# A hybrid decoder layer on one core: the block-sharing product goes ahead of the transposes of L and lv, and half of the masked score copies go behind it

## The chip, the cores and the metric

The kernel runs on one core of one Trainium2 chip. The metric is the time of one execution on the device in microseconds (us). TensorE (PE in the rows) does the matrix products, VectorE (DVE) and ScalarE (ACT) the elementwise work, GpSimd (POOL) the low halves of the split weights, SyncE (SP) issues the loads.

## The reference

One decoder layer over 512 tokens of width 2048: sliding-window attention (16 heads, 4 key/value heads) and RWKV-7 time mixing (16 heads of size 64) beside each other, merged by sigmoid gates, then a SwiGLU feed-forward part and RMS norms. The change lies in the time mixing, whose core is this recurrence:

```python
def step(S, inp):
    r_t, w_t, k_t, v_t, kk_t, a_t = inp
    sa = jnp.einsum('bhij,bhj->bhi', S, -kk_t)
    S = (S * w_t[:, :, None, :] + sa[..., None] * (kk_t * a_t)[:, :, None, :]
         + v_t[..., None] * k_t[:, :, None, :])
    return S, jnp.einsum('bhij,bhj->bhi', S, r_t)
```

## The kernel before

All projections are dense tiles: a weight slot of 128 output channels is split into a high and a low part, and one step of a tile is three products of 128x512 (lines 1362 to 1364), sixteen steps a tile. While these keep TensorE busy, the recurrence is computed in chunked form, for two heads (a pair) at a time, in eight passes over pairs. In each pass the small products of the recurrence are woven in between the dense steps.

For a pair there are four blocks of 128 tokens (t) and two heads (e), so eight units. The parts that matter here, in order, are these:

- The score products ("gram", line 1530): for each unit a product gives a bank of 512 columns with L and three score parts. ScalarE copies L out to `Lt` (line 724, shown as L559 since a helper writes it) and raises `l_read`. VectorE copies the three score parts to `lq` under a mask (line 1124, `copy_predicated`) and raises `g_read`. Units of t = 0 and 1 come first, then two dense steps, then units of t = 2 and 3, which reuse no bank before its copies are done.
- VectorE sums L in blocks of 8 (`block_sums`, lines 1109 and 1117, once for t = 0 and 1 and once for t = 2 and 3), adds a unit matrix (line 1132) and widens the result to `spread` in the buffer `rbuf` (line 1134, raises `spread_ready`).
- TensorE transposes L (line 1541, into `RL`) and forms lv (line 1545, into bank R[1]). It waits for all copies of the scores (`g_read`) and of L (`l_read`) before that. ScalarE copies the results out.
- TensorE multiplies `spread` by `same_block` (line 1552, into bank R[5]) and raises `spread_done`. This is the spreading product. VectorE works through 7 pairs of small operations on it (lines 1143 and 1146) and writes the inverses of the blocks to `Y` (line 1148, raises `base_ready`).
- TensorE starts the first of three levels of the solve (line 1562), for which it waits for `base_ready`. It then transposes (line 1571), and after two dense steps it needs `W1` and `Xc` from ScalarE (line 1582).

The order on each engine is that of its program. How many dense steps stand between two parts is set by the table `FILL` (line 91), which PE, DVE and ACT all read: `fill("solve")` stands behind the second score products, `fill("base")` behind the spreading product. On ScalarE and VectorE a fill does something only where a tile ends. The 16th dense step of a pass ends the first gate tile: ScalarE then splits the next weight slot (`whi`, line 559), applies a sigmoid to the gate tile (line 691), issues its store (line 694), and only then goes to `W1` and `Xc` of the first level. VectorE's evacuation of the gate tile (line 915) stands behind line 1148.

Of the kernel before, what the change touches and what calls it, by code (L numbers as in the profile page):

```python
# [29 lines left out]
P = 128  # L30
D_MODEL, T_SEQ = 2048, 512
KD = D_MODEL // P
HEADS, HD = 16, 64
# [7 lines left out]
NB = T_SEQ // BLOCK  # L41
CHUNK = 64
LEVELS = 5
BASE = 8
# [34 lines left out]
UNITS = 2 * NB  # L79
# [7 lines left out]
for _g in range(STAGES):  # L87
    assert (NB * (sum(ATT_FILL[_g].values()) - ATT_FILL[_g]["first"]) + ATT_FILL[_g]["first"]
            == (FILL_TILE0[_g + 1] - FILL_TILE0[_g]) * KD)

FILL = {"prep": 4, "tok": 3, "gram": 2, "solve": 3, "base": 7, "level_a": 2, "level_b": 1, "join_a": 2, "join_b": 2,
        "rhs": 2, "u": 3, "state": 2, "y": 4}
assert (FILL["prep"] + FILL["tok"] + FILL["gram"] + FILL["solve"] + FILL["base"]
        + SOLVE_LEVELS * (FILL["level_a"] + FILL["level_b"])
        + FILL["join_a"] + FILL["join_b"] + NB * (FILL["rhs"] + FILL["u"] + FILL["state"])
        + FILL["y"]) == 4 * KD
# [31 lines left out]
def build_layer(nc, xT, w_slots, w_ups, w_gu, w_down, norms, pair_cst, low_mu,  # L128
# [5 lines left out]
    V, A, PE = nc.vector, nc.scalar, nc.tensor  # L134
# [25 lines left out]
    start = Arena(nc, front.at)  # L160
# [29 lines left out]
    lq_keep = rw("lq_keep", [3 * P], u8)  # L190
# [3 lines left out]
    kbuf, rbuf, vbuf = (rw(n, [T_SEQ]) for n in ("kbuf", "rbuf", "vbuf"))  # L194
# [5 lines left out]
    lq = rw("lq", [2, NB, 3, P])  # L200
# [9 lines left out]
    lv, rhs, utok = (rw(n, [NB, P]) for n in ("lv", "rhs", "utok"))  # L210
# [3 lines left out]
    upper, same_block = rw("upper", [P]), rw("same_block", [P])  # L214
    block_of, place_in = rw("block_of", [P // BASE]), rw("place_in", [BASE])
    column, partial, inverse = (
        a_in[:, i * UNITS * BASE:(i + 1) * UNITS * BASE].rearrange("p (w n) -> p w n", w=UNITS)
        for i in range(3))
    spread = rbuf[:].rearrange("p (w i k) -> p w i k", w=UNITS, i=BASE)
# [27 lines left out]
    with ExitStack() as ctx:  # L247
        def sem(name):
# [3 lines left out]
        R = [ctx.enter_context(nc.psum_tensor(f"work{i}", [P, T_SEQ], f32)) for i in range(6)]  # L252
# [31 lines left out]
        tok_done, tok_read, g_done, g_read = (  # L284
            sem("tok_done"), sem("tok_read"), sem("g_done"), sem("g_read"))
        xb_read = sem("xb_read")
        l_read = sem("l_read")
        ln_done, ln_read, lv_done, lv_read = (
            sem("ln_done"), sem("ln_read"), sem("lv_done"), sem("lv_read"))
# [5 lines left out]
        g_seen, join_seen = sem("g_seen"), sem("join_seen")  # L295
        spread_ready, spread_done, base_ready = (
            sem("spread_ready"), sem("spread_done"), sem("base_ready"))
# [39 lines left out]
        def g_bank(w):  # L337

            return ((R[3], R[4]), (R[5], R[0]))[w % 2][w // 2 % 2]

        def by_block(ap):
            return ap.rearrange("p (t n) -> p t n", t=NB)
# [16 lines left out]
        def wide(ap, n):  # L359

            return ap.unsqueeze(1).to_broadcast([P, n, ap.shape[-1]])
# [187 lines left out]
        def _(act):  # L549
# [8 lines left out]
            def copy(dst, src, scale=1.0):  # L558
                return A.activation(dst, src, ACT.Copy, scale=scale)  # L559
# [54 lines left out]
            for g in range(STAGES):  # L614
# [4 lines left out]
                fill = Fill(next_tile, ATT_FILL[g])  # L619
# [50 lines left out]
            for i in range(PAIRS // 2):  # L670
                for u in range(2):
                    p = i * 2 + u
# [24 lines left out]
                    fill = Fill(gate_step)  # L697
# [26 lines left out]
                        copy(Lt[:, w % 2, w // 2, :], g_bank(w)[:, 0:P]).then_inc(l_read, 1)  # L724
                    fill("gram")
                    fill("solve")
                    for e in range(2):
                        act.wait_ge(ln_done, p * 2 + e + 1)
                        for c in heads:
                            copy(Ln[c, e], by_block(RL[e][c, :])[:, :, c])  # L730
                        copy(Lcross[heads[1], e], by_block(RL[e][heads[1], :])[:, :, heads[0]]
                             ).then_inc(ln_read, 1)
                    act.wait_ge(lv_done, p + 1)
                    copy(lv[:], by_block(R[1][:])).then_inc(lv_read, 1)
                    fill("base")
                    for level in range(SOLVE_LEVELS):
                        act.wait_ge(w1_done, p * SOLVE_LEVELS + level + 1)
# [2 lines left out]
                        for e in range(2):  # L740
                            done = copy(Xc[heads[e], :, heads[0]], of_head(RX[0], e))
# [6 lines left out]
                    for e in range(2):  # L748
                        done = copy(join_x[heads[e]], R[3][0:CHUNK, e * NB * CHUNK:(e + 1) * NB * CHUNK])
# [91 lines left out]
            for m in range(POOL_OUT):  # L841
                done = copy(resid[:, m, :], resid[:, m, :], norm_g[:, 2, m:m + 1])
# [12 lines left out]
        def _(dve):  # L855
# [85 lines left out]
            for g in range(STAGES):  # L941
# [10 lines left out]
                fill = Fill(next_tile, ATT_FILL[g])  # L952
# [77 lines left out]
            for i in range(PAIRS // 2):  # L1030
                for u in range(2):
                    p = i * 2 + u
# [13 lines left out]
                    fill = Fill(gate_step)  # L1046
# [57 lines left out]
                    def block_sums(h):  # L1104

                        times, parts = slice(2 * h, 2 * h + 2), []
                        for e in range(2):
                            by_place = Y[:, e, times, :].rearrange("p t (i b) -> p t i b", i=BASE)
                            V.tensor_tensor(by_place.rearrange("p t i b -> p t b i"),
                                            Lt[:, e, times, :].rearrange("p t (b i) -> p t b i", i=BASE),  # L1110
                                            upper[:].rearrange("p (b i) -> p b i", i=BASE).unsqueeze(1)
                                            .to_broadcast([P, 2, P // BASE, BASE]), MUL)
                            parts.append(by_place)
                        fence()
                        for e in range(2):
                            at = e * NB + 2 * h
                            V.tensor_reduce(column[:, at:at + 2, :], parts[e], AX, ADD)

                    for t in range(NB):
                        for e in range(2):  # L1120
                            bank = g_bank(2 * t + e)
                            dve.wait_ge(l_read, p * (2 * NB) + 2 * t + e + 1)
                            dve.sem_inc(g_seen, 1)
                            V.copy_predicated(lq[:, e, t].rearrange("p a b -> p (a b)"), lq_keep[:],
                                              bank[:, P:4 * P]).then_inc(g_read, 1)
                        if t == 1:
                            V.tensor_copy(inverse, wide(place_in[:], UNITS))
                            block_sums(0)
                    block_sums(1)
                    units = Y[:].rearrange("p e t n -> p (e t) n")  # L1130
                    fence()
# [2 lines left out]
                    V.tensor_tensor(spread, column.unsqueeze(3).to_broadcast([P, UNITS, BASE, BASE]),  # L1134
                                    place_in[:].unsqueeze(1).unsqueeze(1).to_broadcast(
                                        [P, UNITS, BASE, BASE]), MUL).then_inc(spread_ready, 1)
                    fill("gram")
                    fill("solve")

                    dve.wait_ge(spread_done, p + 1)  # L1140
                    shared = R[5][:].rearrange("p (w i k) -> p w i k", w=UNITS, i=BASE)
                    for n in range(1, BASE):
                        V.tensor_tensor(partial[:, :, 0:n + 1], inverse[:, :, 0:n + 1],
                                        shared[:, :, n, 0:n + 1], MUL)
# [9 lines left out]
                    for at_level, level in enumerate(range(BASE_LEVELS, LEVELS)):  # L1154
                        dve.wait_ge(x_done, p * SOLVE_LEVELS + at_level + 1)
                        for e in range(2):
                            done = V.tensor_copy(Xc[heads[e], :, heads[1]], of_head(RX[1], e))
# [17 lines left out]
                    for e in range(2):  # L1175
                        done = V.tensor_copy(Y[heads[0], e, :, heads[1]], R_half(RP[e])[heads[0]])
# [72 lines left out]
            with dve.Fori(0, KD // 2) as i:  # L1249
                for u in range(2):  # L1250
                    m = i * 2 + u
                    bank = dense[(OUT0 + u) % 2]
# [101 lines left out]
        def _(pe):  # L1354
# [47 lines left out]
            for g in range(STAGES):  # L1402
# [9 lines left out]
                fill = Fill(next_tile, ATT_FILL[g])  # L1412
# [29 lines left out]
                for t in range(NB):  # L1442
                    done = PE.transpose(R[0][:, t * P:(t + 1) * P], vT[g][:, t * P:(t + 1) * P], ident)
                done.then_inc(vt_done, 1)
                fill("first")
                for d in range(NB):
# [14 lines left out]
                    for half in seen:  # L1461
                        for e in range(2):
                            done = PE.matmul(R[5][heads[e], :], vtok[g][:, d - 1 + half, heads[e]],
                                             pT[:, e, half, :], start=(half == seen[0]), stop=(half == 1))
# [4 lines left out]
            for i in range(PAIRS // 2):  # L1469
                for u in range(2):  # L1470
                    p = i * 2 + u
# [15 lines left out]
                    fill = Fill(gate_step)  # L1487
# [20 lines left out]
                    for bank, src in ((R[1], icl), (R[2], kap), (R[0], vbuf)):  # L1508
                        if src is vbuf:
                            pe.wait_ge(shifted, p * 3 + N_LOW + 3)  # L1510
                        for t in range(NB):
                            at = slice(t * P, (t + 1) * P)
                            if src is vbuf:
                                done = PE.matmul(bank[:, at], src[:, at], head_center,
                                                 start=True, stop=True)
                            else:
                                done = PE.transpose(bank[:, at], src[:, at], ident)
# [4 lines left out]
                    for t in range(NB):  # L1522
                        tok = slice(t * P, (t + 1) * P)
# [4 lines left out]
                        for src, half in ((icl, 0), (kap, 2 * P)):  # L1528
                            for e in range(2):
# [3 lines left out]
                                                 start=True, stop=True)  # L1533
                                if src is kap:
                                    done.then_inc(g_done, 1)
                    fill("solve")
                    pe.wait_ge(g_read, (p + 1) * (2 * NB))
                    pe.wait_ge(l_read, (p + 1) * (2 * NB))
                    for e in range(2):
                        for t in range(NB):  # L1540
                            done = PE.transpose(RL[e][:, t * P:(t + 1) * P], Lt[:, e, t, :], ident)
                        done.then_inc(ln_done, 1)
                    for t in range(NB):
                        for e in range(2):
                            done = PE.matmul(R[1][:, t * P + e * HD:t * P + e * HD + HD],
                                             lq[:, e, t, 1, :], vtk[:, t, heads[e]],
                                             start=True, stop=True)
                    done.then_inc(lv_done, 1)


                    pe.wait_ge(spread_ready, p + 1)
                    PE.matmul(R[5][:], same_block[:], rbuf[:], start=True, stop=True
                              ).then_inc(spread_done, 1)
                    fill("base")
                    pe.wait_ge(ln_read, (p + 1) * 2)
                    pe.wait_ge(base_ready, p + 1)
# [340 lines left out]
```

## Time and profile before

| what | value |
|---|---|
| median of 3 runs | 2911.03 us (2910.7 to 2914.75) |
| time of the profiled execution | 2912.67 us |
| its span | 2910.9 us |
| TensorE busy | 2870.2 us, 99% |
| VectorE, ScalarE, GpSimd busy | 929.1, 927.9, 1268.4 us |
| mean granted clock of TensorE | 0.997 of full speed |

The span is the stretch that the profile shows; 1.8 us of the execution's own time lie outside it. A busy TensorE is one with a matmul in flight, so time in which a matmul drains into a wait counts as busy.

### The profile page before, as it was taken

How to read it: one execution, taken by the hardware profiler on the slowest of the kernel's cores; microseconds unless marked ns; L12 is line 12 of the kernel's file. 1: busy time of each engine (PE TensorE's matmuls, PEld its weight loads, DVE VectorE, ACT ScalarE, POOL GpSimd, SP SyncE). 2: the span in 40 equal slices, each digit the busy share in tenths (PEclk: the TensorE clock that was granted, in tenths of full speed). 3: DMA queues.
4: the chain of work that ended last, by engine and by line, in shares of the span. 5: the costliest groups of instructions: out<-in, count | busy, mean ns of one | idle time of the engine just before them, and what ended most of it. 6: DMA issues, size and time to landing. Idle time of an engine off the chain costs nothing.

```text
span 2910.9 us, 38148 instructions
## 1 busy us (share of the span) xinstructions
PE 2870.2 (99%) x14821; PEld 2327.1 (80%) x14821; DVE 929.1 (32%) x1495; ACT 927.9 (32%) x1182; POOL 1268.4 (44%) x1027
## 2 busy tenths in 40 slices
PE   8999999999999999999999999999999999999998
PEld 7767777777777778888888888888888888888887
DVE  5666456456456454233321110111101111011122
ACT  5443333333333333222233322333123331222222
POOL 2333323323323325555554444454454454444454
PEclk9999999999999999999999999999999999999999
DMA  5212222222222224333343223222232222322223
GB/s 180 73 73 100 86 77 84 83 79 84 85 78 84 86 103 150 150 144 132 145 148 115 96 80 112 99 89 96 89 103 100 101 84 94 110 94 94 92 89 108
DMA packets 65692, 296.14 MB, mean 102 GB/s; under 512 B 6849, under 2 KB 12225, under 8 KB 41409
## 3 DMA queue, kind: packets, MB, share of 16 engines
q1 hardware_dynamic: 57632, 280.17, 27.3%
q10 hardware_dynamic: 7968, 14.68, 1.3%
q8 instruction: 65, 1.06, 0.2%
q14 instruction: 27, 0.21, 0.0%
HBM read 274.12 MB, written 20.71 MB: 101 GB/s over the span
## 4 chain that ended last, share of the span: by engine, by line
PE 92%; DVE 3%; ACT 2%; issue 1%; DVEq 1%; DMA 0%; POOL 0%; ACTq 0%; SPq 0%; POOLq 0%
PE dense L1362 27%; PE dense L1364 26%; PE dense L1363 26%; PE work L1530 1%; DVEq L862 1%; PE work L1582 1%; PE work L1364 0%; PE work L1362 0%; PE work L1363 0%; ACT whi L559 0%; PE dense L1680 0%; PE work L1680 0%; PE work L1685 0%; PE work L1681 0%; PE dense L1685 0%
## 5 line engine op out<-in xcount | busy, mean ns | idle before, releaser
L513 POOL TENSOR_TENSOR wlo<-raw,whi 128x512 fp32r<-128x512 f32 (+1 forms) x1008 | 1255.6, 1277 | 1622.8 <-ACT whi L559 1622.8
L1362 PE MATMUL dense<-H_hi,whi 128*128 128x512 f32 x2616 | 1053.0, 403 | 11.0 <-DVE H_lo L890 9.6
L1364 PE MATMUL dense<-H_hi,wlo 128*128 128x512 f32 x2616 | 1020.8, 390 | 0.0
L1363 PE MATMUL dense<-H_lo,whi 128*128 128x512 f32 x2616 | 1020.6, 390 | 0.0
L559 ACT ACTIVATE whi<-raw 128x2048 fp32r<-128x2048 f32 (+2 forms) x261 | 455.6, 1747 | 1520.0 <-PE dense L1364 1434.8
L1362 PEld LDWEIGHTS dense<-H_hi,whi 128*128 128x128 f32 x2616 | 491.9, 188 | 138.1 <-issue 27.2
L1364 PEld LDWEIGHTS dense<-H_hi,wlo 128*128 128x128 f32 x2616 | 491.6, 188 | 104.9
L1363 PEld LDWEIGHTS dense<-H_lo,whi 128*128 128x128 f32 x2616 | 492.2, 188 | 99.6 <-issue 6.0
L1362 PE MATMUL dense<-G_hi,whi 128*128 128x512 f32 x693 | 269.6, 389 | 0.0
L1363 PE MATMUL dense<-G_lo,whi 128*128 128x512 f32 x693 | 269.6, 389 | 0.0
L1364 PE MATMUL dense<-G_hi,wlo 128*128 128x512 f32 x693 | 269.6, 389 | 0.0
L1279 DVE TENSOR_TENSOR hid<-rstd,dense 128x512 f32<-128x512 f32 x44 | 30.2, 687 | 443.3 <-PE dense L1364 443.3
L1291 DVE TENSOR_TENSOR resid<-resid,dense 128x512 f32 (+1 forms) x63 | 43.3, 688 | 385.6 <-PE dense L1364 385.6
L1364 PEld LDWEIGHTS dense<-G_hi,wlo 128*128 128x128 f32 x693 | 130.1, 188 | 27.1
L1363 PEld LDWEIGHTS dense<-G_lo,whi 128*128 128x128 f32 x693 | 130.1, 188 | 27.0
L1362 PEld LDWEIGHTS dense<-G_hi,whi 128*128 128x128 f32 x693 | 130.1, 188 | 26.9
L1276 DVE TENSOR_TENSOR gate_n<-rstd,dense 128x512 f32<-128x512 f32 x44 | 30.2, 687 | 312.4 <-PE dense L1364 311.9
L1362 PE MATMUL dense<-M_hi,whi 128*128 128x512 f32 x256 | 99.6, 389 | 0.0
L1363 PE MATMUL dense<-M_lo,whi 128*128 128x512 f32 x256 | 99.6, 389 | 0.0
L1364 PE MATMUL dense<-M_hi,wlo 128*128 128x512 f32 x256 | 99.6, 389 | 0.0
L1284 DVE TENSOR_TENSOR G_lo<-hid,G_hi 128x512 f32 x44 | 54.9, 1247 | 42.9 <-ACT G_hi L559 42.9
L559 ACT ACTIVATE Lt<-work 128x128 f32<-128x128 f32 (+2 forms) x136 | 41.4, 329 | 74.5 <-PE work L1530 44.5
(294 smaller groups left out, 2343.2 us busy)
## 6 DMA issues: line engine op xcount, KB each, us to landing
raw<-w_slots SPq DMA_DIRECT2D x101, 1024.0 KB, 4.9
raw<-w_gu SPq DMA_DIRECT2D x88, 1024.0 KB, 4.7
raw<-w_down SPq DMA_DIRECT2D x64, 704.0 KB, 4.0
gates_dram<-gout ACTq DMA_DIRECT2D x32, 256.0 KB, 2.1
gin<-gates_dram SPq DMA_DIRECT2D x16, 512.0 KB, 3.8
X<-xT SPq DMA_DIRECT2D x8, 512.0 KB, 9.8
xin<-xT SPq DMA_DIRECT2D x16, 256.0 KB, 3.6
x_dram<-x ACTq DMA_DIRECT2D x16, 256.0 KB, 3.8
```

The source lines that it names most:

```text
L513: done = nc.gpsimd.tensor_tensor(wlo[s][:, at], raw[s][:, at], whi[s][:, at].bitcast(f32), SUB)
L559: return A.activation(dst, src, ACT.Copy, scale=scale)
L862: V.drain()
L1276: V.tensor_tensor(gate_n[:], rstd[:], dense[s][:], MUL).then_inc(bank_read, 1)
L1279: V.tensor_tensor(hid[:], rstd[:], dense[1 - s][:], MUL).then_inc(bank_read, 1)
L1284: V.tensor_tensor(tile_of(G_lo, t), hid[:], tile_of(G_hi, t).bitcast(f32), SUB).then_inc(g_lo_ready, 1)
L1291: V.tensor_tensor(tile_of(resid, m), tile_of(resid, m), dense[s][:], ADD).then_inc(bank_read, 1)
L1362: PE.matmul(bank[:], whi[s][:, wk], hi[:, k, :], start=(k == first), stop=False)
L1363: PE.matmul(bank[:], whi[s][:, wk], lo[:, k, :], start=False, stop=False)
L1364: done = PE.matmul(bank[:], wlo[s][:, wk], hi[:, k, :], start=False, stop=(k == last))
L1530: done = PE.matmul(g_bank(2 * t + e)[:, half:half + 2 * P], src[heads[e], tok], zq[heads[e], t].rearrange("p a n -> p (a n)"), start=True, ...
L1582: done = PE.matmul(RP[e][heads[c], first_col:first_col + HALF // 2], Xc[heads[e], t, heads[c]], W1[heads[e], t, c * (HALF // 2):(c + 1) * ...
```

## The change

Three things move. On TensorE the spreading product goes ahead of the transposes of L and the products for lv; a new fill of two steps (`spread`) stands between them, `solve` has 4 steps in place of 3 and `base` 4 in place of 7. On VectorE the four masked score copies of t = 2 and 3 stand behind `spread`, and the second `block_sums` has a wait of its own for all eight copies of L. Banks R[1] and R[5] change places for the spreading product and lv.

```diff
-FILL = {"prep": 4, "tok": 3, "gram": 2, "solve": 3, "base": 7, "level_a": 2, "level_b": 1, "join_a": 2, "join_b": 2,
+FILL = {"prep": 4, "tok": 3, "gram": 2, "solve": 4, "spread": 2, "base": 4, "level_a": 2, "level_b": 1, "join_a": 2, "join_b": 2,
...
                     fill("solve")
+                    fill("spread")
...
                     act.wait_ge(lv_done, p + 1)
-                    copy(lv[:], by_block(R[1][:])).then_inc(lv_read, 1)
+                    copy(lv[:], by_block(R[5][:])).then_inc(lv_read, 1)
...
-                    for t in range(NB):
-                        for e in range(2):
-                            bank = g_bank(2 * t + e)
-                            dve.wait_ge(l_read, p * (2 * NB) + 2 * t + e + 1)
-                            dve.sem_inc(g_seen, 1)
-                            V.copy_predicated(lq[:, e, t].rearrange("p a b -> p (a b)"), lq_keep[:],
-                                              bank[:, P:4 * P]).then_inc(g_read, 1)
-                        if t == 1:
-                            V.tensor_copy(inverse, wide(place_in[:], UNITS))
-                            block_sums(0)
+                    def keep_scores(times):
+
+                        for t in times:
+                            for e in range(2):
+                                bank = g_bank(2 * t + e)
+                                dve.wait_ge(l_read, p * (2 * NB) + 2 * t + e + 1)
+                                dve.sem_inc(g_seen, 1)
+                                V.copy_predicated(lq[:, e, t].rearrange("p a b -> p (a b)"), lq_keep[:],
+                                                  bank[:, P:4 * P]).then_inc(g_read, 1)
+
+                    keep_scores((0, 1))
+                    V.tensor_copy(inverse, wide(place_in[:], UNITS))
+                    block_sums(0)
+                    dve.wait_ge(l_read, (p + 1) * (2 * NB))
                     block_sums(1)
...
                                         [P, UNITS, BASE, BASE]), MUL).then_inc(spread_ready, 1)
+                    keep_scores((2, 3))
                     fill("gram")
                     fill("solve")
+                    fill("spread")
 
                     dve.wait_ge(spread_done, p + 1)
-                    shared = R[5][:].rearrange("p (w i k) -> p w i k", w=UNITS, i=BASE)
+                    shared = R[1][:].rearrange("p (w i k) -> p w i k", w=UNITS, i=BASE)
...
                     fill("solve")
+                    pe.wait_ge(spread_ready, p + 1)
+                    PE.matmul(R[1][:], same_block[:], rbuf[:], start=True, stop=True
+                              ).then_inc(spread_done, 1)
+                    fill("spread")
                     pe.wait_ge(g_read, (p + 1) * (2 * NB))
...
-                            done = PE.matmul(R[1][:, t * P + e * HD:t * P + e * HD + HD],
+                            done = PE.matmul(R[5][:, t * P + e * HD:t * P + e * HD + HD],
...
-                    pe.wait_ge(spread_ready, p + 1)
-                    PE.matmul(R[5][:], same_block[:], rbuf[:], start=True, stop=True
-                              ).then_inc(spread_done, 1)
                     fill("base")
```

The order of TensorE before, in the first pass, from the last score products (line 1530) to the first level (line 1562). The rows of lines 1362 to 1364 are dense steps, of which one stands for each fill (3, then 7):

```order
L1530 MATMUL work<-zq,kap 128x256 x2
L1362 MATMUL dense<-H_hi,whi_53 128x512
...
L1541 MATMUL work<-cst,Lt 128x128 [waits l_read,g_read]
L1541 MATMUL work<-cst,Lt 128x128 x7
L1545 MATMUL work<-vtk,lq 128x64 x8
L1552 MATMUL work<-rbuf,same_block 128x512 [waits spread_ready]
L1362 MATMUL dense<-H_hi,whi_53 128x512
...
L1362 MATMUL dense<-H_hi,whi_54 128x512 [waits evacuated,lo_ready]
...
L1562 MATMUL work<-Y,Ln 64x64 [waits base_ready,ln_read]
```

The same place of the changed kernel, whose lines are numbered 7 to 11 higher (line 1545 is the spreading product, 1552 the transposes of L, 1556 lv, 1570 the first level). The fills have 4, 2 and 4 steps:

```order
L1537 MATMUL work<-zq,kap 128x256 x2
L1369 MATMUL dense<-H_hi,whi_53 128x512
...
L1545 MATMUL work<-rbuf,same_block 128x512 [waits spread_ready]
L1369 MATMUL dense<-H_hi,whi_53 128x512
...
L1552 MATMUL work<-cst,Lt 128x128 [waits l_read,g_read]
L1552 MATMUL work<-cst,Lt 128x128 x7
L1556 MATMUL work<-vtk,lq 128x64 x8
L1369 MATMUL dense<-H_hi,whi_53 128x512
...
L1369 MATMUL dense<-H_hi,whi_54 128x512 [waits evacuated,lo_ready]
...
L1570 MATMUL work<-Y,Ln 64x64 [waits base_ready,ln_read]
```

The spreading product moved up past the transposes and lv, with one dense step more ahead of it; between the score products and the row with `whi_54` (the first step of the next tile) there are 7 dense steps in both orders, and 3 from there to the first level.

The order of VectorE before, in the same pass, from the masked score copies to the first of the small operations:

```order
L1124 COPY_PREDICATED lq<-lq_keep,work 128x384 [waits l_read] x4
L1127 COPY a_in<-place_in 128x64
L1109 TENSOR_TENSOR Y<-Lt,upper 128x2x16x8 x2
L1117 TENSOR_REDUCE a_in<-Y 128x16 x2
L1124 COPY_PREDICATED lq<-lq_keep,work 128x384 [waits l_read] x4
L1109 TENSOR_TENSOR Y<-Lt,upper 128x2x16x8 x2
L1117 TENSOR_REDUCE a_in<-Y 128x16 x2
L1132 TENSOR_TENSOR a_in<-a_in,place_in 128x64
L1134 TENSOR_TENSOR rbuf<-a_in,place_in 128x512
L1143 TENSOR_TENSOR a_in<-a_in,work 128x8x2 [waits spread_done]
```

And in the changed kernel:

```order
L1127 COPY_PREDICATED lq<-lq_keep,work 128x384 [waits l_read] x4
L1131 COPY a_in<-place_in 128x64
L1110 TENSOR_TENSOR Y<-Lt,upper 128x2x16x8 x2
L1118 TENSOR_REDUCE a_in<-Y 128x16 x2
L1110 TENSOR_TENSOR Y<-Lt,upper 128x2x16x8 [waits l_read]
L1110 TENSOR_TENSOR Y<-Lt,upper 128x2x16x8
L1118 TENSOR_REDUCE a_in<-Y 128x16 x2
L1137 TENSOR_TENSOR a_in<-a_in,place_in 128x64
L1139 TENSOR_TENSOR rbuf<-a_in,place_in 128x512
L1127 COPY_PREDICATED lq<-lq_keep,work 128x384 [waits l_read] x4
L1150 TENSOR_TENSOR a_in<-a_in,work 128x8x2 [waits spread_done]
```

The second four copies moved from ahead of the second block sums to behind `spread`, and the second block sums wait for `l_read` themselves.

## Rows read from the trace of the kernel before

**Rows 1.** The page: engines, and shares of the chain that ended last.

```profile
PE 2870.2 (99%) x14821; PEld 2327.1 (80%) x14821; DVE 929.1 (32%) x1495; ACT 927.9 (32%) x1182; POOL 1268.4 (44%) x1027
...
PE 92%; DVE 3%; ACT 2%; issue 1%; DVEq 1%; DMA 0%; POOL 0%; ACTq 0%; SPq 0%; POOLq 0%
```

**Rows 2.** Waits of TensorE, 265 to 1062 us: total, times, longest.

```profile
PE work L1562 <- DVE Y L1148: 4.0, 8, 0.8
...
PE work L1582 <- ACT Lt L559: 0.9, 5, 0.3
```

**Rows 3.** Chain that ended last, fifth pass: start, us, what.

```profile
726.93 0.24 PE dense L1364
...
727.25 1.92 ACT whi L559
...
729.18 1.28 ACT L691
730.48 0.64 ACT gout L691
...
732.61 0.74 PE work L1582 x32
```

**Rows 4.** Timeline of TensorE, fifth pass: start, us, engine, line, what [idle before].

```profile
718.56 0.50 PE L1362 MATMUL dense<-H_hi,whi 128*128 128x512 f32 x1
718.90 0.40 PE L1363 MATMUL dense<-H_lo,whi 128*128 128x512 f32 x1
...
720.73 1.04 PE L1541 MATMUL work<-cst,Lt 128*128 128x128 f32 x8
...
723.34 1.08 PE L1552 MATMUL work<-rbuf,same_block 128*128 128x512 f32 x2
...
724.49 0.40 PE L1363 MATMUL dense<-H_lo,whi 128*128 128x512 f32 x1
...
728.80 0.39 PE L1364 MATMUL dense<-H_hi,wlo 128*128 128x512 f32 x1
729.62 0.69 PE L1562 MATMUL work<-Y,Ln 128*64 128x64 f32 x16 [0.43 <-DVE Y L1148]
```

**Rows 5.** Timeline of VectorE, fifth pass.

```profile
714.70 1.99 DVE L1124 COPY_PREDICATED lq<-lq_keep,work 128x384 f32<-128x384 uint8 x4 [4.62 <-ACT Lt L559]
...
717.78 0.75 DVE L1117 TENSOR_REDUCE a_in<-Y 128x16 f32<-128x256 f32 x2
718.44 1.99 DVE L1124 COPY_PREDICATED lq<-lq_keep,work 128x384 f32<-128x384 uint8 x4
720.32 1.03 DVE L1109 TENSOR_TENSOR Y<-Lt,upper 128x256 f32<-128x256 f32 x2
...
722.55 0.69 DVE L1134 TENSOR_TENSOR rbuf<-a_in,place_in 128x512 f32<-128x512 f32 x1
724.46 0.17 DVE L1143 TENSOR_TENSOR a_in<-a_in,work 128x16 f32<-128x16 f32 x1 [1.22 <-PE work L1552]
...
728.25 1.23 DVE L1148 TENSOR_TENSOR Y<-a_in,block_of 128x1024 f32<-128x1024 f32 x1
```

**Rows 6.** Timeline of ScalarE, fifth pass: copies of L to Lt.

```profile
714.27 0.45 ACT L559 ACTIVATE Lt<-work 128x128 f32<-128x128 f32 x2 [2.51 <-PE work L1530]
...
718.66 0.45 ACT L559 ACTIVATE Lt<-work 128x128 f32<-128x128 f32 x2 [0.42 <-PE work L1530]
```

**Rows 7.** Timeline of TensorE, second pass.

```profile
402.32 0.69 PE L1562 MATMUL work<-Y,Ln 128*64 128x64 f32 x16 [0.75 <-DVE Y L1148]
...
405.09 0.67 PE L1582 MATMUL work<-W,Lt 64*64 64x32 f32 x32
```

**Rows 8.** Stretches: length; PE, PEld, DVE, ACT, POOL busy; granted clock; DMA.

```profile
266.00:270.00 4.00, 0.97 (x5) 0.51 (x4) 3.92 (x4) 0.00 (x0) 3.93 (x3) 0.94 0.21 86
270.00:274.00 4.00, 4.00 (x19) 2.83 (x19) 3.54 (x4) 1.20 (x2) 2.48 (x2) 0.64 0.13 25
728.00:732.00 4.00, 3.57 (x43) 2.72 (x42) 2.83 (x5) 3.56 (x5) 2.76 (x3) 1.00 0.03 7
```

More of the change, by code:

```diff
@@ L89 @@
             == (FILL_TILE0[_g + 1] - FILL_TILE0[_g]) * KD)
-FILL = {"prep": 4, "tok": 3, "gram": 2, "solve": 3, "base": 7, "level_a": 2, "level_b": 1, "join_a": 2, "join_b": 2,
+FILL = {"prep": 4, "tok": 3, "gram": 2, "solve": 4, "spread": 2, "base": 4, "level_a": 2, "level_b": 1, "join_a": 2, "join_b": 2,
         "rhs": 2, "u": 3, "state": 2, "y": 4}
-assert (FILL["prep"] + FILL["tok"] + FILL["gram"] + FILL["solve"] + FILL["base"]
+assert (FILL["prep"] + FILL["tok"] + FILL["gram"] + FILL["solve"] + FILL["spread"] + FILL["base"]
         + SOLVE_LEVELS * (FILL["level_a"] + FILL["level_b"])
```

## The prediction

> **What bounds the kernel.** I first read the page. TensorE is busy 99% of the span and makes up 92% of the chain that ended last [rows 1], so any microsecond in which TensorE stands still in the eight passes over pairs is a microsecond of the result, and time on VectorE or ScalarE counts only through such a stop. Then I read the waits of TensorE in that stretch. Two are near the change: the first level of the solve waits for the inverses of the blocks (`Y`, line 1148) in all eight passes, 4.0 us in sum, and the product behind it (line 1582) waits for ScalarE's copies, 0.9 us in five [rows 2]. The change seems aimed at the first. The third view, the chain in order of time, says that the first is not what sets the end of the stage. In the fifth pass the chain does not run through `Y`. It leaves TensorE at the end of the 16th dense step (727.17), goes through ScalarE's split of the next weight slot, a table load, the sigmoid and the store of the gate tile, to `W1` and `Xc`, and comes back at line 1582 at 732.61 [rows 3]. That is 5.44 us of ScalarE work hung on the 16th dense step. The reader should see that there are two chains side by side, and that the wait for `Y` only fills time in which TensorE would have waited for ScalarE two steps later.
>
> **What moves, and what it costs.** The number of instructions is the same on every engine; only order and waits differ. I take the fifth pass as the pattern, and all times are starts from its rows.
>
> *When `spread` is ready.* Before, the second block sums start at 720.32 and `spread` (line 1134) ends at 722.55 + 0.69 = 723.24, so 2.92 us for this piece [rows 5]. After, the first block sums end at 718.53, but the second now need all eight copies of L, and the last of these ends at 718.66 + 0.45 = 719.11 [rows 6]. The handover from ScalarE to VectorE takes about 0.15: the first pair of copies of L starts at 714.27 and takes 0.45, the second of the two starts some 0.17 later, so the first is done near 714.55, and VectorE starts at 714.70 [rows 5, 6]. The second block sums then start at 719.26 and `spread` is ready at 722.18. That is 1.06 earlier, not the 1.88 that the four copies took away would suggest (718.44 to 720.32): the rest turns into VectorE's wait for `l_read`.
>
> *When TensorE wants it.* Three dense steps go from 718.56 to 720.73, and a further one takes 0.69 (the pitch of a product is 0.23) [rows 4], so after four steps TensorE stands at the spreading product at 721.42. It is released at 722.18 + 0.08 = 722.26. The 0.08 is an estimate, half of the handover above; before, TensorE started 0.10 after `spread` was done without a listed wait, so it can't be much more. **That is a new stop of 0.84 us in each pass.** Everything behind it on TensorE's queue waits too, the two dense steps included. Before, the product came at 723.34, behind the transposes and lv, and found `spread` done [rows 4, 5].
>
> *The copies behind `spread`.* They overlap it by 0.10 and take 1.99 [rows 5], so they end at 722.08 + 1.99 = 724.07. TensorE needs them for the transposes after the product (723.34 to the next dense pitch at 724.27, or 0.93) and two steps (1.37), at 724.56 [rows 4]. They are 0.49 early and cost nothing; if they were later than that, every further tenth would be a tenth in each pass.
>
> *One more change of kind.* The step from lv back to dense products is new (before, lv ran into the spreading product). Behind the score products the first dense product takes 0.34 to the next start in place of 0.23 (718.56 to 718.90) [rows 4], and it begins about 0.1 late. No row shows a 128x64 product ahead of a dense one, so I bound it by 0 below and by 0.21 above, and take 0.15, nearer to the upper end because the score products are the nearest row.
>
> *The 16th dense step.* The transposes and lv take 2.61 (720.73 to 723.34). They start at 724.56 and end at 727.17, with 0.15 the dense pitch goes on at 727.32, and one step more ends the tile at 728.01. Before, it was the fourth step after 724.27, at 727.0. The 16th step is 1.0 us later, of which 0.84 is the stop and 0.15 the change of kind.
>
> *The wait for `Y`.* The spreading product ends at 722.26 + 1.08 = 723.34, VectorE is still at the copies until 724.07, and from the first small operation to the end of `Y` it takes 729.48 - 724.46 = 5.02 [rows 5]. `Y` is ready at about 729.1. TensorE comes there three steps after 728.01, at 730.05. The wait is gone: before, the dense products ended their pitch at 728.80 + 0.23 = 729.03 and line 1562 started at 729.62 [rows 4], which is 0.59 us lost (the listed 0.43 leaves out the drain). In the second and sixth pass 0.75 is listed, so about 0.91 is lost [rows 7].
>
> *Where it is given back.* ScalarE's chain hangs on the 16th step and keeps its length, so `Xc` is done 1.0 later, and line 1582 starts at 733.6 in place of 732.61. TensorE would be there at 732.9: it waits 0.7 where it waited 0.15. In the second and sixth pass line 1582 had some 0.1 to spare (no wait is listed there [rows 7]), which takes 0.1 off each. ScalarE's own copy of lv would end at about 727.95, ahead of the 16th step, so the chain is not lengthened by it.
>
> The sum is 8 x 1.0 - 2 x 0.1 = **+7.8 us**. Against the profiled execution of 2912.67 us (span 2910.9 and 1.8 around it) that is 2920.5. That execution lies 1.6 above the median of the runs, and for the median I predict 2911.03 + 7.8 = **2918.8 us**, or 0.27% slower. 0.2% (5.8 us) is about what a measurement of this kernel can tell from no change.
>
> **A rule that speaks against the change.** In the first pass a long stop of TensorE is followed by a granted clock of 0.94 and then 0.64 in the next 4 us, while the stretch with the stop at line 1562 kept 1.00 [rows 8]. The granted clock has two levels, 1.2 and 2.4 GHz, so 0.64 is a mixture of the two. If the new stop brought this in each pass, it would cost (0.06 + 0.36) x 4 = 1.7 us more each. The Trainium skill, page TensorE: Matmul & The Clock Gate, section What's actually happening, says that recent activity of the array sets its clock, so that a new stop can cost more than its length; by that rule the sum would be 7.8 + 13.6. The trace agrees with it for the long stop. For stops of the new one's size it shows none, and I keep the sum without it.
>
> **The rivals.**
>
> - *Only the net at line 1562 counts.* If ScalarE's chain were not tied to the 16th step, TensorE would lose 1.0 and win back 0.59 in six passes, and lose 1.0 and win back 0.91 in two: 6 x 0.41 + 2 x 0.09 = +2.6, 2913.6 us. For it speaks that line 1582 lists only 0.9 us of wait [rows 2]; against it, that the chain shows ScalarE without a gap from the 16th step on [rows 3]. Chance 0.13.
> - *The spreading product finds `spread` ready.* This needs `spread` 0.84 earlier than I have it. Then the 0.15 alone stays: +1.2, 2912.2 us. The wait for the last copy of L speaks against it. Chance 0.06.
> - *The copies come too late for the transposes.* This needs VectorE to be 0.8 behind my count at the end of the copies; with the 0.49 used up, each pass loses 0.3 more: +2.4 on top, 2921.2 us. No row speaks for it, but the copies have never stood behind `spread`. Chance 0.05.
> - *The clock falls,* as above: 2932.4 us. Chance 0.02.
> - *The other side: faster.* The wait for `Y` falls away (6 x 0.59 + 2 x 0.91 = 5.4) and so does that at line 1582 (0.9): -6.3, 2904.7 us. It decides if `spread` is in time and ScalarE's chain gets at least 0.2 shorter, for instance because VectorE's evacuation of the gate tile, now earlier, had held the sigmoid. Against it: the sigmoid starts 0.02 after the table load ends [rows 3], so nothing else held it. Chance 0.04.
>
> That the change does not do what it says is excluded, since the order of the two engines shows both moves.
>
> **How the numbers follow.** The forecast has 0.70, the rivals 0.13, 0.06, 0.05, 0.02 and 0.04. The forecast's own bounds: the change of kind at 0 or 0.21 gives 6.6 or 8.3; the handovers may be off by 0.1 each way, which is 0.8 for each; so 5.8 to 9.1. The range reaches down to the first rival and up past the third, 2913.4 to 2922.5. Slower by over 0.2%: the forecast (less 0.03 for its lower end), the late copies and the clock, 0.74. Within 0.2%: 0.13 + 0.06 + 0.03 = 0.22. Faster: 0.04.
>
> **What would show it.** In the profile of the changed kernel TensorE should wait for `rbuf` at the spreading product in all eight passes, by about 0.8 (some 0.65 as listed, since the drain counts as busy). VectorE should show a gap of 0.7 ahead of the second block sums, put down to ScalarE's copies of L. The wait for `Y` at the first level should be gone, and that for ScalarE's `Lt` at the product two steps later should be near 0.7 in each pass. No wait for `lq` should stand at the transposes. The weakest steps are the first and the last: a shorter stop at the spreading product takes its full amount off the 16th step, and if the wait at the level's second product does not grow, the first rival was right.

## The result, and the profile after

| what | before | changed |
|---|---|---|
| median of 20 runs | 2911.7 us | 2918.18 us (2916.45 to 2922.44) |
| ratio to the kernel before | | 1.0022 [1.0016, 1.0028] |
| span of the profiled execution | 2910.9 us | 2915.2 us |

The changed kernel is slower by 0.22% (the interval goes from 0.16 to 0.28%), or 6.4 us. The forecast was +7.8 us.

First the waits of TensorE in the eight passes of the changed kernel (engine, line and tile that waited, what it waited for: total, times, longest):

```profile
PE work L1590 <- ACT Lt L559: 5.1, 8, 0.7
PE work L1545 <- DVE rbuf L1139: 4.9, 8, 0.9
```

The wait for `Y` at the first level of the solve, 4.0 us before [rows 2], is no longer in the list. In its place stands a wait of the spreading product for `rbuf` (4.9 us) and the wait for `Lt` at the product after the first level grew from 0.9 to 5.1 us. Both come in all eight passes.

The fifth pass shows how they hang together. The timeline of TensorE (start, us, engine, line, what [idle before, and what ended it]), to be read against [rows 4]:

```profile
719.34 0.50 PE L1369 MATMUL dense<-H_hi,whi 128*128 128x512 f32 x1
...
721.97 0.39 PE L1371 MATMUL dense<-H_hi,wlo 128*128 128x512 f32 x1
722.92 1.13 PE L1545 MATMUL work<-rbuf,same_block 128*128 128x512 f32 x2 [0.56 <-DVE rbuf L1139]
...
725.26 1.03 PE L1552 MATMUL work<-cst,Lt 128*128 128x128 f32 x8
726.13 1.90 PE L1556 MATMUL work<-vtk,lq 128*128 128x64 f32 x16
727.84 0.48 PE L1369 MATMUL dense<-H_hi,whi 128*128 128x512 f32 x1
728.15 0.39 PE L1370 MATMUL dense<-H_lo,whi 128*128 128x512 f32 x1
...
730.78 0.69 PE L1570 MATMUL work<-Y,Ln 128*64 128x64 f32 x16
...
734.24 0.67 PE L1590 MATMUL work<-W,Lt 64*64 64x32 f32 x32 [0.62 <-ACT Lt L559]
```

VectorE in the same pass, against [rows 5]:

```profile
719.92 1.06 DVE L1110 TENSOR_TENSOR Y<-Lt,upper 128x256 f32<-128x256 f32 x2 [0.62 <-ACT Lt L559]
...
722.17 0.69 DVE L1139 TENSOR_TENSOR rbuf<-a_in,place_in 128x512 f32<-128x512 f32 x1
722.78 1.98 DVE L1127 COPY_PREDICATED lq<-lq_keep,work 128x384 f32<-128x384 uint8 x4
...
728.43 1.23 DVE L1155 TENSOR_TENSOR Y<-a_in,block_of 128x1024 f32<-128x1024 f32 x1
```

And ScalarE. The gap ahead of `whi` is the wait for the 16th dense step:

```profile
719.44 0.45 ACT L559 ACTIVATE Lt<-work 128x128 f32<-128x128 f32 x2 [0.42 <-PE work L1537]
...
728.06 0.60 ACT L559 ACTIVATE lv<-work 128x512 f32<-128x512 f32 x1
728.88 1.92 ACT L559 ACTIVATE whi<-raw 128x2048 fp32r<-128x2048 f32 x1 [0.21 <-PE dense L1371]
730.81 1.28 ACT L691 ACT_TABLE_LOAD   x1
732.10 0.63 ACT L691 ACTIVATE gout<-gout 128x512 f32<-128x512 f32 x1
...
733.43 0.75 ACT L559 ACTIVATE Lt<-work 64x256 f32<-64x256 f32 x2
```

A reader should measure everything from one mark (in what follows, "the mark"), the first dense product after the second score products (718.56 before, 719.34 after), since the passes begin at different times. From that mark `spread` is ready at 4.68 before and 3.52 after. TensorE reaches the spreading product after four steps, at 2.63 + 0.23 = 2.86 (the last product starts at 721.97, and the next could follow one pitch, 0.23, later), and starts it at 3.58: a stop of 0.72. The row lists 0.56, because the last product runs for 0.39, 0.16 longer than its pitch, and that drain counts as busy. ScalarE's split starts at 8.69 before and 9.54 after, and the product after the first level at 14.05 before and 14.90 after. The same 0.85 stands at both ends of ScalarE's chain, which runs from the split without a long gap to the copies for that product.

Summed over the eight passes, the time from this mark to that product is 113.3 us before and 119.7 us after: +6.4 us. From there to the mark of the next pass it is 95.0 us in both kernels, in every pass. So the whole measured loss lies in the stage that was edited. The spans differ by only 4.3 because the mark of the first pass came 2.0 us earlier in the profiled execution of the changed kernel (at 279.66 against 281.70), which the last section takes up.

### The profile page after: what moved, and what is told of

Read it like the earlier page. It is cut to its first block, busy times and chain, and to the rows that moved or that the text cites. A ratio compares the mean times of both kernels' runs of the same rounds, so it can differ in the third digit from the quotient of the medians.

```text
span 2915.2 us, 38148 instructions
## 1 busy us (share of the span) xinstructions
PE 2869.0 (98%) x14821; PEld 2323.8 (80%) x14821; DVE 928.1 (32%) x1495; ACT 928.0 (32%) x1182; POOL 1267.4 (43%) x1027
## 3 DMA queue, kind: packets, MB, share of 16 engines
q8 instruction: 65, 1.06, 0.1%
## 4 chain that ended last, share of the span: by engine, by line
PE 91%; DVE 3%; ACT 2%; issue 1%; DVEq 1%; DMA 0%; POOL 0%; ACTq 0%; SPq 0%; POOLq 0%
PE dense L1369 27%; PE dense L1370 26%; PE dense L1371 26%; PE work L1537 1%; DVEq L863 1%; ACT whi L559 1%; PE work L1590 1%; PE work L1371 0%; PE work L1369 0%; PE work L1370 0%; PE work L1556 0%; PE dense L1688 0%; PE work L1688 0%; PE work L1693 0%; PE work L1689 0%
```

## The experiments

Each was timed in five rounds beside the kernel before. A difference in us that stands beside a ratio is that ratio times the median of the kernel before. Where a stage time is given, it is that from the mark to the product after the first level, and the rest is the time from there to the next mark.

**1. The changed kernel, ScalarE's gate work behind the first level.** ScalarE alone is edited:

```diff
-                    fill("base")
                     for level in range(SOLVE_LEVELS):
...
                         done.then_inc(x_read, 1)
+                        if level == 0:
+                            fill("base")
                         fill("level_a")
```

> The changed kernel, with one edit on ScalarE alone: the base fill (split of the next weight slot, table load, sigmoid, store of the gate tile) stands behind the copies W1 and Xc of the first level instead of ahead of them. Theory (the stop at the spreading product moves the 16th dense step, and ScalarE's chain that hangs on it sets when the second product of the level can start): the wait for Lt at that product goes (5.1 us in 8 passes), it starts 2.77 us after the first level in place of 3.46, the stage gets 0.7 us shorter in each pass, and the kernel is 5.6 us faster than the changed one, 0.8 us above the kernel before (+0.03%). The stop at the spreading product (4.9 us listed) stays. Rival (only the net at the first level counts, ScalarE's chain is not what holds): nothing changes, it stays 6.4 us above the kernel before (+0.22%).

Measured: 2914.44 us, ratio 1.0011 [1.0002, 1.0020], or +3.2 us over the kernel before. The timeline of TensorE in the fifth pass:

```profile
723.19 1.12 PE L1546 MATMUL work<-rbuf,same_block 128*128 128x512 f32 x2 [0.57 <-DVE rbuf L1140]
...
731.06 0.69 PE L1571 MATMUL work<-Y,Ln 128*64 128x64 f32 x16
...
733.83 0.67 PE L1591 MATMUL work<-W,Lt 64*64 64x32 f32 x32
...
738.50 0.67 PE L1591 MATMUL work<-W,Lt 64*64 64x32 f32 x32 [0.20 <-ACT Lt L559]
```

The wait at the product after the first level is gone, and it starts 2.77 after the level, as forecast (14.22 from the mark in place of 14.90, 5.6 us in sum). The stop at the spreading product is the same. So it was ScalarE's chain that held that product, and the first rival falls. What I had not seen is the last row: the moved work now delays the copies of the second level, and the rest of a pass grows from 95.0 to 95.28. 5.6 - 8 x 0.28 = 3.4 us gained by the trace. The forecast for the whole, +0.8 us, missed this price; 6.4 - 3.4 = 3.0 agrees with the measured 3.2.

**2. The kernel before with the same edit.**

> The kernel before with the same edit on ScalarE. Theory: the wait for Y at the first level stays (4.0 us listed, 0.59 us really lost in six passes and 0.91 in two), the wait for Lt behind it (0.9 us listed) goes, and the kernel gets 1.5 us faster (-0.05%). Rival: no change.

Measured: 2913.45 us, ratio 1.0004 [0.9995, 1.0013]. In the waits:

```profile
PE work L1563 <- DVE Y L1149: 4.0, 8, 0.8
...
PE work L1583 <- ACT Lt L559: 1.6, 8, 0.2
```

The stage got 1.4 us shorter in sum (forecast 1.5). The 0.28 in the rest of each pass costs 2.2, so the trace gives +0.8, where the time gives +1.2 (-1.5 to +3.8). The 1.6 us listed for `Lt` is now that of the second level. The forecast for the whole was wrong for the same reason as in 1, and the time alone would settle nothing here.

**3. Five steps ahead of the spreading product, one behind.**

```diff
-FILL = {"prep": 4, "tok": 3, "gram": 2, "solve": 4, "spread": 2, "base": 4, "level_a": 2, "level_b": 1, "join_a": 2, "join_b": 2,
+FILL = {"prep": 4, "tok": 3, "gram": 2, "solve": 5, "spread": 1, "base": 4, "level_a": 2, "level_b": 1, "join_a": 2, "join_b": 2,
```

> The changed kernel with 5 dense steps ahead of the spreading product and 1 behind it (4 and 2 before). Theory (the stop at the spreading product is a wait for spread, 0.73 us in a pass): it shrinks to about 0.05, a new stop of 0.2 to 0.25 appears at the transposes of L, which now come before the masked copies are done, and the stage gets 0.47 us shorter: 3.8 us faster than the changed kernel, +2.6 us over the kernel before (+0.09%). Rival (most of the stop is the price of breaking into the dense products a second time, not a wait): the stop keeps its size and the kernel stays at +6.4 us (+0.22%).

Measured: 2915.74 us, ratio 1.0012 [1.0003, 1.0021], or +3.5 us. The fifth pass:

```profile
722.60 1.13 PE L1545 MATMUL work<-rbuf,same_block 128*128 128x512 f32 x2
...
724.03 0.40 PE L1371 MATMUL dense<-H_hi,wlo 128*128 128x512 f32 x1
724.50 1.09 PE L1552 MATMUL work<-cst,Lt 128*128 128x128 f32 x8
...
733.54 0.67 PE L1590 MATMUL work<-W,Lt 64*64 64x32 f32 x32 [0.62 <-ACT Lt L559]
```

The product still starts 3.58 after the mark (719.02), with one step more done ahead of it, so the stop was a wait for `spread` and not a price of the switch. The new stop at the transposes is 0.24: the dense products end their pitch at 724.03 + 0.23 = 724.26 (the last of them starts at 724.03), and the transposes start at 724.50. The drain hides all but 0.08 of it, and it is not listed as idle time of the products; the list of weight loads, which sit idle longer, has it:

```profile
PEld work L1552 <- DVE lq L1127: 4.1, 8, 0.5
```

The stage takes 14.52 in place of 14.90, in sum 3.1 us less than in the changed kernel; 6.4 - 3.1 = 3.3 us over the kernel before agrees with the time. The forecast had the stage 0.47 us shorter in a pass; it got 0.38 shorter.

**4. TensorE's half of the change alone.**

```diff
                     block_sums(0)
+                    keep_scores((2, 3))
...
                                         [P, UNITS, BASE, BASE]), MUL).then_inc(spread_ready, 1)
-                    keep_scores((2, 3))
```

> TensorE's half of the change alone: the spreading product goes ahead of the transposes, but VectorE makes all eight masked copies ahead of spread, as before. Theory: spread is ready 4.7 us after the second score products and TensorE is there after 2.85, so the stop is 1.9 us in each pass in place of 0.73; the kernel is 9.2 us slower than the changed one, +15.6 us over the kernel before (+0.54%). Rival (TensorE's new order costs only the change of kind, and VectorE's new wait for the copies of L is what hurts): about +1.2 us over the kernel before (+0.04%).

Measured: 2927.15 us, ratio 1.0056 [1.0042, 1.0069], or +16.3 us. TensorE lists 14.3 us for `rbuf`:

```profile
731.63 1.12 PE L1545 MATMUL work<-rbuf,same_block 128*128 128x512 f32 x2 [1.75 <-DVE rbuf L1140]
```

It starts 4.76 after the mark (726.87), and `Lt` is waited for 5.1 us in sum as in the changed kernel. The stop passes on in full (the stage takes 16.09 in this pass, 1.18 more than in the changed kernel, and the stop is 1.90 in place of 0.72; in sum it is 15.8 us over the kernel before), and the arithmetic of the forecast holds at a stop more than twice as long.

**5. VectorE's half alone.** TensorE has the order of before again (solve 3, spread 0, base 7):

```diff
                     fill("solve")
-                    pe.wait_ge(spread_ready, p + 1)
-                    PE.matmul(R[1][:], same_block[:], rbuf[:], start=True, stop=True
-                              ).then_inc(spread_done, 1)
-                    fill("spread")
...
                     done.then_inc(lv_done, 1)
+                    pe.wait_ge(spread_ready, p + 1)
+                    PE.matmul(R[1][:], same_block[:], rbuf[:], start=True, stop=True
+                              ).then_inc(spread_done, 1)
```

> VectorE's half of the change alone: the four late masked copies stand behind spread, while TensorE keeps the order of before (3 dense steps, transposes of L, lv, spreading product, 7 dense steps; the banks are those of the changed kernel). Theory: the transposes wait for the copies, which end 5.4 us after the second score products, while TensorE is there after 2.2: a stop of 3.3 us in each pass, no wait at the spreading product, and everything behind it 3.3 us later, since ScalarE's chain hangs on the 16th step: +26 us over the kernel before (+0.9%). Rival (only what the spreading product waits for matters, and spread is ready earlier): no slower than the kernel before.

Measured: 2952.03 us, ratio 1.0152 [1.0138, 1.0166], or +44 us by the ratio and 40.5 by the medians. In the third pass the stop is what was forecast:

```profile
516.79 1.09 PE L1548 MATMUL work<-cst,Lt 128*128 128x128 f32 x8 [3.13 <-DVE lq L1127]
```

The stage takes 17.4 to 17.8 us in five passes, 3.3 us more than before in the mean. But in the first, fourth and fifth it takes 22.3, 21.8 and 20.7. The stretches behind the stop (length; busy time of PE, PEld, DVE, ACT, POOL; granted clock; DMA) show why, first the third pass, then the fourth:

```profile
516.00:524.00 8.00, 7.21 (x42) 6.11 (x43) 3.27 (x15) 3.26 (x8) 0.00 (x0) 1.00 0.01 2
...
629.00:637.00 8.00, 7.84 (x29) 6.62 (x30) 0.62 (x4) 2.65 (x7) 0.00 (x0) 0.50 0.01 2
```

In the long passes the granted clock fell to 0.50 of full speed, which is 1.2 in place of 2.4 GHz. Against the 17.5 of the other passes these three lose 4.8, 4.3 and 3.2 us, 12.3 in sum. The profiled execution, the shortest of the five, took 2949.75, which is 38.2 over the median of the kernel before, or 12.2 over the forecast of 26. So the fourth rival of the prediction is real behind some stops of 3.1 us; behind the stops that the change makes it did not show.

**6. The kernel before, one dense step moved into the wait for Y.**

```diff
-FILL = {"prep": 4, "tok": 3, "gram": 2, "solve": 3, "base": 7, "level_a": 2, "level_b": 1, "join_a": 2, "join_b": 2,
-        "rhs": 2, "u": 3, "state": 2, "y": 4}
+FILL = {"prep": 4, "tok": 3, "gram": 2, "solve": 3, "base": 8, "level_a": 2, "level_b": 1, "join_a": 2, "join_b": 2,
+        "rhs": 2, "u": 3, "state": 2, "y": 3}
```

> The kernel before with one dense step moved from the fill y (4 to 3) to the fill base (7 to 8), so that the step lies in the wait for Y at the first level instead of at the end of the pass, where no wait is listed. Order of all other work as before. Theory: the 16th dense step and ScalarE's chain keep their place, the second product of the level still starts 14.1 us after the second score products, one step of 0.69 more is done by then, and the step is saved at the end of the pass, if three steps cover what four did there: -5.5 us (-0.19%). Rival (the wait for Y is on the path by itself, and a step ahead of it delays the level as much as it saves later): no change; or the fill y was needed, and a new wait of up to 0.7 us a pass stands at the last product of the pass: no change either, with that wait listed.

Measured: 2908.26 us, ratio 0.9989 [0.9980, 0.9998], or -3.2 us, the only version here that beats the kernel before. The fifth pass, whose mark is 716.01:

```profile
726.96 0.39 PE L1364 MATMUL dense<-H_hi,wlo 128*128 128x512 f32 x1
727.27 0.69 PE L1562 MATMUL work<-Y,Ln 128*64 128x64 f32 x16
...
730.08 0.67 PE L1582 MATMUL work<-W,Lt 64*64 64x32 f32 x32
```

The stage ends at 14.07, where it ended before, with a step more inside, and neither of the two waits is listed. The rest of a pass is 94.28 in place of 95.00, so three steps in the fill y are enough. By the trace that is -5.6 us; the time gives -3.2, and its interval (-5.8 to -0.6) holds both.

**7. The changed order with its waits filled.** FILL has solve 5, spread 1, base 5 and y 3.

> The changed order with its waits filled: 5 steps ahead of the spreading product, 1 behind it, base 5, y 3. Theory: as with 5, 1 and 4 the second product of the level starts 14.5 us after the second score products (ScalarE's chain), the wait for Lt there (0.7 us a pass) is filled by the step, and the end of the pass saves 0.69: against the kernel before 8 x (0.36 - 0.69) = -2.6 us (-0.09%), so still some 3 us behind the order of before with the same filling. Rival (the changed order is at least as good once its waits are filled): as fast as or faster than the kernel before with base 8 and y 3.

Measured: 2910.64 us, ratio 0.9998 [0.9989, 1.0007]. The stage takes 14.5 to 14.6 (14.87 in the seventh pass) and the rest 94.29, which is -2.4 us by the trace and within the interval of the time. No wait for `Lt` is listed. The order of before with the same step is some 2.4 us ahead in the medians and 3.1 in the stages; the two intervals overlap, so the times by themselves do not separate the two, and the stage sums do. Only this one table of fills was tried for the changed order with y at 3; that no table makes it better than the order of before is not shown.

## Why the prediction was right

**The wait for Y was not what set the end of the stage: right.** It is gone, and the stage is longer. In experiment 1 an edit of ScalarE's order alone takes the wait at the next product away, so it is ScalarE's chain that holds it. In 6 a step put into the wait for `Y` costs nothing at the other end.

**spread 1.06 us earlier, at 3.62 from the mark: nearly.** It was ready at 3.52, 1.16 earlier. The 0.15 for the handover from ScalarE to VectorE was too much: `Lt` ends at 719.44 + 0.45 = 719.89 and VectorE starts at 719.92. The rest of that piece took 2.94, against 2.92. That the second block sums would wait for the copies of L is shown by the 0.62 in their row.

**A new stop of 0.84: right in place, 0.72 in size.** The shorter handover makes up the difference. As listed it is 0.56, against my 0.65. Experiment 3 shows that it is a wait, and 4 that it scales with the lateness of `spread`.

**The copies behind spread are hidden: right.** They end at 5.42 from the mark, the transposes start at 5.92, and no wait for `lq` is listed. Experiment 3 brought TensorE there 0.69 earlier, so that the cover of 0.50 was gone, and a stop of 0.24 appeared; 5 brought it there 3.7 earlier, and a stop of 3.3 us appeared.

**The change of kind, 0.15: too large.** The dense product behind lv starts at 727.84, 0.31 ahead of the next, so about 0.08 is lost. The lower half of the bound would have been nearer.

**The 16th step 1.0 later, and the same at the product after the first level: 0.85 at both.** The difference to the forecast is 0.12 less at the stop and 0.07 less at the change of kind, with 0.03 more in the spreading product itself. ScalarE's copy of lv ends at 728.66, 0.22 ahead of its split, so it does not lengthen the chain. `Y` was ready at 10.32 from the mark and TensorE came for it at 11.44. In the second and sixth pass the slack took off a little more than the forecast 0.1 (the passes are 0.73 and 0.68 longer than before). Those are the passes in which VectorE stands still for 0.43 to 0.45 us ahead of the end of `Y`; that made the wait for `Y` longer there before, and the changed kernel, which comes for `Y` later, does not see it.

**The sum, +7.8: +6.4 measured.** 8 x 0.85 = 6.8, less 0.7 in the passes whose stage was longer before (0.36 of it in the third, which had a hole on VectorE, the rest mostly in the second and sixth), plus 0.3 in the seventh, where VectorE now had a hole of 0.42 ahead of `spread`. That hole was the only thing like the third rival, and it lies at the spreading product, not at the transposes. The first rival, the net at the first level (+2.6), is refuted by 1 and by the stage sums, and so is the faster kernel; the second, `spread` in time, by the stop of 0.72; the fourth by the granted clock of 1.00 behind all the new stops.

## What to carry to other kernels

When two chains end close together on the engine that bounds the kernel, shortening the one that has a wait listed only moves that wait to the other. Follow the chain that ended last through the stage, find the event on which it hangs (here the end of the 16th dense step), and ask of each move whether this event comes earlier or later. Here it was cheaper to put independent work into the short wait, behind that event, than to reorder the dependence. And a table of fills tuned for one order has to be tuned again for another before the two orders are compared.

## What the runs showed of the hardware

**The same stop halves the clock in some passes and not in others.** In experiment 5 TensorE stood still for 3.1 us as listed in each pass (3.5 in the seventh); the granted clock behind it was 1.00 in the third and 0.50 in the fourth, with the same instructions around it. Behind the stops of 0.7 us of the changed kernel and of 1.9 us in experiment 4 it stayed at 1.00 in all passes. The first row is the changed kernel, the second experiment 4:

```profile
30.00:2910.00 2880.00, 2848.36 (x14737) 2306.68 (x14735) 906.85 (x1463) 905.87 (x1148) 1267.17 (x1023) 1.00 0.28 99
...
275.00:2910.00 2635.00, 2611.52 (x13584) 2126.06 (x13583) 751.68 (x1141) 799.42 (x915) 1167.66 (x943) 1.00 0.28 99
```

In the kernel before, the stop of 3.03 us at line 1507 ahead of the first pass was followed by 0.94 and 0.64 [rows 8]. In the profiled execution of the changed kernel that stop fell apart in two, 1.7 and 1.4 us, and the clock stayed at 1.00:

```profile
266.00:270.00 4.00, 2.00 (x10) 1.23 (x10) 3.76 (x4) 0.69 (x2) 4.00 (x3) 1.00 0.00 0
270.00:274.00 4.00, 2.94 (x17) 2.50 (x17) 1.69 (x2) 0.99 (x2) 2.13 (x2) 1.00 0.21 43
```

Experiment 1 has the same two stops and also stays at 1.00:

```profile
266.00:270.00 4.00, 2.27 (x10) 1.53 (x9) 3.85 (x5) 1.19 (x1) 2.73 (x2) 1.00 0.48 201
270.00:274.00 4.00, 2.64 (x19) 1.96 (x18) 3.44 (x4) 1.08 (x2) 4.00 (x3) 1.00 0.00 0
```

The other six experiments have one long stop of 3.1 to 3.4 us there, and between 266 and 274 us the clock falls in all of them. From the last small product ahead of that stop (it starts at 252.04 before, 251.32 in the changed kernel, 253.24 in experiment 1) to the first mark it is 29.66, 28.34 and 28.35 us, and 29.8 to 30.4 in the other six. So 1.3 of the 2.0 us by which the first mark of the changed kernel came earlier lie in this stretch and go with the split stop and the full clock; the other 0.7 lie ahead of it. Nothing in the change touches that place, and in experiment 1 the first mark came at 281.59, about as late as before. What splits the stop is not shown.

**VectorE stands still for about 0.42 us at fixed instructions.** The row of such a hole in the seventh pass of the changed kernel, put down to nothing that the profile shows, and behind it the same operation in the third pass of the kernel before:

```profile
941.19 0.75 DVE L1118 TENSOR_REDUCE a_in<-Y 128x16 f32<-128x256 f32 x2 [0.42 <-issue]
...
503.31 0.75 DVE L1117 TENSOR_REDUCE a_in<-Y 128x16 f32<-128x256 f32 x2 [0.42 <-issue]
```

The hole is in the seventh pass in all five kernels in which VectorE makes the late copies behind `spread` (the changed one and experiments 1, 3, 5 and 7), and in the third in all four in which it makes them ahead (the kernel before and experiments 2, 4 and 6). The spreading product comes 0.31 to 0.36 later in that pass than in the undisturbed ones. The edits to ScalarE, to TensorE's order and to the fills did not move it; VectorE's order did. Five more holes of 0.41 to 0.45 us between 250 and 870 us come at the same operations in all nine profiles. What causes them stays open.
